# A block with two attentions: normed heads and squared activations kept in PSUM, V made tile by tile, two result banks

## The chip, the core and the metric

The kernel runs on one core of a Trainium2 chip. The metric is device time in microseconds (us) of one execution. TensorE (PE) multiplies and writes to PSUM, VectorE (DVE), ScalarE (ACT) and GpSimd (POOL) do the elementwise work, and SyncE (SP) starts the transfers. PSUM has 8 banks of 128 x 512 float32; GpSimd works in SBUF only.

## The reference

All values are float32, 512 tokens, width 1024. Cut to what matters here:

```python
# first block: layer 0 is a short convolution beside an attention, layer 1 a convolution module
def squared_relu_mlp(h, w1, w2):                 # once in each of the two layers, width 4096
    return jnp.square(jax.nn.relu(h @ w1)) @ w2

# second block: one layer, 16 meta tokens ahead of the 512
proj = _rmsnorm(h) @ w_in                        # q, k, v (8 heads of 64), forget gate, u (512)
q, k = _rmsnorm(q per head, q_norm_w), _rmsnorm(k per head, k_norm_w)
log_f = jax.nn.log_sigmoid(fg + b_fgate); cum_logf = jnp.cumsum(log_f)
s = q @ k.T * HEAD_DIM ** -0.5 + cum_logf[t] - cum_logf[s]     # causal
a_out = softmax(s) @ v                           # by query blocks of 128
pooled = trailing means of u over 2, 4, 8, 16 tokens, minus u   # one window per 128 columns
p_out = einsum(pooled, w_pool) * pool_scale
h = h + concat([a_out, p_out]) @ w_out
h = h + (silu(n2 @ w_gate) * (n2 @ w_up)) @ w_down              # width 2816
```

## The kernel before

**Layout.** Activations are held transposed: features on the 128 partitions, 512 tokens in the free dimension. A weight block is 8 tiles of 128 x 128. Each float32 operand is split into two parts of TensorE's rounded type (`wh`/`wl`, `XH`/`XL`, `HH`/`HL`, and so on): ScalarE or VectorE rounds (high part), and a subtraction gives the low part. A product is three matmuls (high x high, high x low, low x high; lines 1478 to 1480). A tile of 8 k-steps is 24 matmuls and fills one of the banks 0 to 3 in turn.

**Order.** It is written by hand, engine by engine, and held together by semaphores; each engine runs its own list in order. Weights pass through a ring of four slots: SP loads block n, ScalarE makes `wh` (`hi(n)`, which waits for the block n-3 counted by `blocks_done`), GpSimd makes `wl` (`lo_range`), PE multiplies. `bank_free` counts the tiles whose bank VectorE has read.

**The squared-ReLU MLP** (twice, each in two chunks of 16 tiles up and 8 down). For each up tile VectorE runs four instructions (lines 1207 to 1213): `tmp0 = PSUM * r2`; `tmp1 = max(tmp0, 0) * tmp0`; a cast `tmp1` to `HH`; `HL = tmp1 - HH`. The second half of the first down tile needs all 16 up tiles (`hid`).

**w_in_2** (the second block's input projection). Tiles 0 to 3 are q, 4 the forget gate, 5 to 8 u, 9 the first k tile; then the pool products (12 matmuls), then three k tiles, then V. A k or q tile is two heads. For head pair e: `head_in` scales the tile into `head_t`, ScalarE squares it, PE sums by head (`head_stat`, line 1779), ScalarE takes the root, VectorE inverts and spreads the factors (`hexp`), PE turns them into bank HB (`head_spread`, line 1788), and `head_norm` multiplies in place and writes both parts of both heads (`Q2H`, `Q2L`, `K2H`, `K2L`). `head_stat(e)` waits until pair e-1 is finished (`heads_done`). The hooks of `tile` put stats and spreads between the k-steps of a later tile. Tiles 4 to 9 and the k tiles also multiply the 16 meta tokens (48 short matmuls more). V runs k-step by k-step over four banks at once, and 20 matmuls without use (`keep_busy`) stand ahead of the attention.

**The second attention** runs in 32 units (head h, query block i) through a pipeline in which step s does scores(s), transposes unit s-3 (`turn`) and multiplies by V every other step (`values`). ScalarE: exponent of s, then copies of the transposed unit s-3, and for s = 9, 13, ... the copy `XH` of a finished head (line 755). VectorE: maximum, reciprocal, low parts, and `XL` of the head (line 937, followed by `yl_done`). GpSimd normalises. There is one result bank, so `values` of the next head waits for `yl_done`; the weights of the first four tiles of w_out_2 are made before it.

## Time and profile before

| | us |
|---|---|
| median of 3 runs (1941.9 to 1943.06) | 1942.8 |
| the profiled execution | 1945.64 |
| its span, first to last instruction | 1943.9 |
| PE busy (95% of the span) | 1848.9 |
| DVE, POOL, ACT busy | 1009.1, 921.5, 579.1 |

Matmuls are pipelined, and a row's duration includes the overlap: in a row of matmuls with 512 columns they start 0.23 us apart though each lasts 0.39. Stages of the span, in us: first attention about 180 to 246, MLP 0 about 300 to 490 in its first chunk, MLP 1 about 930 to 1110, w_in_2 about 1285 to 1453, the second attention 1457.9 to 1528.7, w_out_2 and the gated MLP from there.

### The profile page before, as it was taken

What the parts mean: (1) busy time and instruction counts of PE and PEld (TensorE: products, weight loads), DVE (VectorE), ACT (ScalarE), POOL (GpSimd) and SP (SyncE); (2) the same over time, 40 slices, a digit from 0 to 9 for tenths busy, and PEclk for the clock granted to TensorE, in tenths of its full rate; (3) what the DMA queues carried; (4) which work ended last, traced back from release to release, by engine and by line L of the source; (5) the groups of instructions that cost most, each with busy time, mean ns of one, the idle gap of its engine ahead of it and who ended that gap; (6) DMA issues with size and microseconds to landing.
All of it is one profiled execution on the core that took longest, in us unless ns stands there. A gap on an engine that the chain in (4) does not pass through costs nothing.

```text
span 1943.9 us, 23828 instructions
## 1 busy us (share of the span) xinstructions
PE 1848.9 (95%) x8563; PEld 1527.0 (79%) x8563; DVE 1009.1 (52%) x1330; ACT 579.1 (30%) x854; POOL 921.5 (47%) x482
## 2 busy tenths in 40 slices
PE   7897999999999999899999999999898999999999
PEld 5776977878888777677878888888778778888887
DVE  4886737820771479856770384257526335444300
ACT  4225714111111444344211111142126342222221
POOL 7345535434444469935534444452224354444442
PEclk9998999999999999999999999999889999999999
DMA  5152022323332213202322233321110023323332
GB/s 180 48 141 76 1 70 72 97 87 97 97 96 93 71 54 96 80 31 87 98 86 97 97 95 96 95 72 50 51 45 12 33 75 100 96 96 97 98 107 76
DMA packets 45782, 157.87 MB, mean 81 GB/s; under 512 B 5585, under 2 KB 5841, under 8 KB 45713
## 3 DMA queue, kind: packets, MB, share of 16 engines
q1 hardware_dynamic: 45712, 156.93, 25.6%
q8 instruction: 46, 0.75, 0.2%
q14 instruction: 24, 0.19, 0.0%
HBM read 152.58 MB, written 2.10 MB: 80 GB/s over the span
## 4 chain that ended last, share of the span: by engine, by line
PE 73%; DVE 17%; POOL 5%; issue 3%; ACT 1%; DMA 0%; DVEq 0%; SPq 0%; POOLq 0%; ACTq 0%
PE PS L1478 23%; PE PS L1479 22%; PE PS L1480 22%; DVE HL L937 2%; DVE tmp L945 2%; PE PS L1488 2%; POOL acc_p L519 2%; DVE HH L1211 2%; POOL wl L508 2%; DVE tmp L937 1%; DVE sqb L937 1%; PE PS L1649 1%; POOL acc_p L551 1%; PE PS L1508 1%; PE PS L1788 1%
## 5 line engine op out<-in xcount | busy, mean ns | idle before, releaser
L451 POOL TENSOR_TENSOR wl<-raw,wh 128x1024 fp32r<-128x1024 f32 x240 | 593.0, 2473 | 764.7 <-ACT wh L606 484.9
L1478 PE MATMUL PS<-XH,wh 128*128 128x512 f32 x1440 | 577.0, 401 | 32.0 <-DVE XL L945 16.2
L1479 PE MATMUL PS<-XL,wh 128*128 128x512 f32 x1440 | 566.7, 394 | 0.0
L1480 PE MATMUL PS<-XH,wl 128*128 128x512 f32 x1440 | 566.5, 393 | 0.0
L606 ACT ACTIVATE wh<-raw 128x1024 fp32r<-128x1024 f32 x152 | 161.1, 1061 | 668.1 <-PE PS L1480 668.1
L1478 PEld LDWEIGHTS PS<-XH,wh 128*128 128x128 f32 x1440 | 274.0, 190 | 100.8 <-issue 23.2
L1480 PEld LDWEIGHTS PS<-XH,wl 128*128 128x128 f32 x1440 | 273.9, 190 | 58.4
L1479 PEld LDWEIGHTS PS<-XL,wh 128*128 128x128 f32 x1440 | 274.3, 190 | 53.4
L1478 PE MATMUL PS<-HH,wh 128*128 128x512 f32 x688 | 269.6, 392 | 8.4 <-DVE HL L937 8.4
L1479 PE MATMUL PS<-HL,wh 128*128 128x512 f32 x688 | 269.1, 391 | 0.0
L1480 PE MATMUL PS<-HH,wl 128*128 128x512 f32 x688 | 268.8, 391 | 0.0
L937 DVE TENSOR_TENSOR tmp<-PS,r 128x512 f32<-128x512 f32 x126 | 86.8, 691 | 144.2 <-PE PS L1480 118.7
L1478 PEld LDWEIGHTS PS<-HH,wh 128*128 128x128 f32 x688 | 130.1, 189 | 36.5 <-POOL wl L451 9.2
L592 ACT ACTIVATE wh<-raw 128x1024 fp32r<-128x1024 f32 x94 | 98.5, 1055 | 195.9 <-PE PS L1480 179.9
L1480 PEld LDWEIGHTS PS<-HH,wl 128*128 128x128 f32 x688 | 130.1, 189 | 27.2
L1479 PEld LDWEIGHTS PS<-HL,wh 128*128 128x128 f32 x688 | 130.2, 189 | 26.8
L1211 DVE CAST HH<-tmp 128x512 f32 x64 | 110.2, 1721 | 9.6 <-DVE tmp L945 5.8
L1231 DVE COPY M<-PS 128x512 f32 x16 | 11.1, 692 | 158.4 <-PE PS L1480 158.4
L442 POOL TENSOR_TENSOR wl<-raw,wh 128x1024 fp32r<-128x1024 f32 x20 | 48.9, 2451 | 90.4 <-ACT wh L592 90.2
L916 ACT ACTIVATE wh<-raw 128x1024 fp32r<-128x1024 f32 x40 | 42.5, 1062 | 158.4 <-PE PS L1480 158.4
L472 POOL TENSOR_TENSOR prob<-prob,cols 128x512 f32<-128x512 f32 (+2 forms) x64 | 57.5, 900 | 66.6 <-DVE cols L1138 66.3
L937 DVE TENSOR_TENSOR X<-X,PS 128x512 f32<-128x512 f32 x16 | 11.0, 688 | 148.4 <-PE PS L1480 148.4
(277 smaller groups left out, 2326.8 us busy)
## 6 DMA issues: line engine op xcount, KB each, us to landing
raw<-weights SPq DMA_DIRECT2D x286, 512.0 KB, 3.5
X<-x_t SPq DMA_DIRECT2D x8, 256.0 KB, 6.8
out_t<-X SPq DMA_DIRECT2D x8, 256.0 KB, 4.6
KH<-rope_h SPq DMA_DIRECT2D x4, 128.0 KB, 4.5
KL<-rope_l SPq DMA_DIRECT2D x4, 128.0 KB, 5.4
QH<-XH SPq DMA_DIRECT2D x16, 32.0 KB, 2.0
QL<-XL SPq DMA_DIRECT2D x16, 32.0 KB, 2.0
pos_i<-positions SPq DMA_DIRECT2D x1, 256.0 KB, 8.2
```

The costliest lines, as they stand in the source:

```text
L442: pool.tensor_tensor(wl[:, n % RING], raw[:, n % RING], wh[:, n % RING].bitcast(F32), ALU.subtract).then_inc(w_lo, 1)
L451: pool.tensor_tensor(wl[:, j], raw[:, j], wh[:, j].bitcast(F32), ALU.subtract).then_inc(w_lo, 1)
L472: pool.tensor_tensor(p, p, cols[:, u % 4, 2:3].broadcast_to(p.shape), ALU.mult).then_inc(p_done, 1)
L508: pool.tensor_tensor(wl[:, i % RING], raw[:, i % RING], wh[:, i % RING].bitcast(F32), ALU.subtract).then_inc(w_lo, 1)
L592: sc.activation(wh[:, j], raw[:, j], ACT.Copy).then_inc(w_hi, 1)
L606: sc.activation(wh[:, j], raw[:, j], ACT.Copy).then_inc(w_hi, 1)
L916: sc.activation(wh[:, slot], raw[:, slot], ACT.Copy).then_inc(w_hi, 1)
L937: return v.tensor_tensor(out, a, b, op)
L1211: v.tensor_copy(HH[:, g * 4 + j], tmp[:, 1]).then_inc(dve, 1)
L1478: pe.matmul(out, wa, xa, start=start, stop=False)
L1479: pe.matmul(out, wa, xb, start=False, stop=False)
L1480: return pe.matmul(out, wb, xa, start=False, stop=stop)
```

## The change

1. **MLPs.** ScalarE keeps the square of `r2` (only for entries x1 and x3). VectorE: `tmp0 = PSUM * r2`; `x = max(PSUM, 0) * tmp0`, written to PSUM (banks 6 and 7 in turn), which frees the tile's bank; ScalarE copies `x` to `HH`; VectorE: `HL = x - HH`. ScalarE's loop holds the weight's `hi` and the `HH` copy in turn.
2. **Heads.** `head_norm` is split in three: `head_factor`, `head_norm` (one multiplication that leaves the normed pair in bank HB, `head_n`) and `head_low`. ScalarE writes the high parts (`head_round`), VectorE only the low parts. `head_stat(e)` waits for `head_n`, `head_spread(e)` for `heads_done` of pair e-1. VectorE's list interleaves these with the forget gate and the pool tiles; the low parts of the pooled tiles go to GpSimd.
3. **w_in_2 order.** The second k tile moves ahead of the pool products; hooks move.
4. **V** is made one tile after the other, the meta product after the second; `v_done` releases each. The 20 matmuls and the wait for all four V tiles ahead of the attention are gone.
5. **Attention.** Results alternate between banks 6 and 7; the small transposed part moves to the bank of the main part, or to bank 5.
6. **w_out_2.** Its first four `hi` and `lo` are put into the attention, at steps 13, 17, 21 and 25 of ScalarE and ahead of GpSimd's units 12, 16, 20 and 24.

```diff
+W_OUT_2_STEPS = (13, 17, 21, 25)
+        def squared(j):
+            return PS[:, (HB, META_BANK)[j % 2]]
-                    PS[0:META, (5, 7)[u % 2], 0:P])
+            small = PS[0:META, 5, 0:P] if i == 3 else PS[0:META, (4, 1)[u % 2], S - (i % 2 + 1) * P:S - i % 2 * P]
-            return 6 + h % 2 if layer == 0 else 6
+            return 6 + h % 2
# gpsimd, normalise(layer)
+                    if layer == 1 and u + 1 in W_OUT_2_STEPS:
+                        n = BLOCK0["w_out_2"] + W_OUT_2_STEPS.index(u + 1)
+                        lo_range(n, n + 1)
# gpsimd, w_in_2
-            lo_range(BLOCK0["w_in_2"] + 4, BLOCK0["w_in_2b"] + 7)
+            for t in range(4):
+                lo_range(BLOCK0["w_in_2"] + (9 + t if t else 4), BLOCK0["w_in_2"] + 10 + t)
+                pool.wait_ge(pool_hi, t + 1)
+                pool.tensor_tensor(pool_l[:, t], pooled[:, t], pool_h[:, t].bitcast(F32), ALU.subtract)
...
# scalar
+                form = ACT.Square if entry in ("x1", "x3") else ACT.Copy
+                    if layer == 1 and s in W_OUT_2_STEPS:
+                        hi(BLOCK0["w_out_2"] + W_OUT_2_STEPS.index(s))
+                    if c == 0:
+                        for j in range(4):
+                            sc.wait_ge(bank_free, T0 + j + 1)
+                            sc.activation(HH[:, j], squared(j), ACT.Copy).then_inc(hid_hi, 1)
+                    with sc.Fori(1 if c == 0 else 0, CHUNK // 4, 1) as g:
...
+                            sc.activation(wh[:, slot], raw[:, slot], ACT.Copy).then_inc(w_hi, 1)
+                            sc.wait_ge(bank_free, g * 4 + (T0 + j + 1))
+                            sc.activation(HH[:, g * 4 + j], squared(j), ACT.Copy).then_inc(hid_hi, 1)
+            def head_round(e):
+                sc.wait_ge(head_n, e + 1)
+                for odd in range(2):
+                    sc.activation(H[:, tokens], PS[:, HB], ACT.Copy, scale=own).then_inc(head_hi, 1)
# vector, mlp
-                            tt(tmp[:, 0], PS[:, (T0 + j) % 4], r2[:], ALU.mult).then_inc(bank_free, 1)
-                            stt(tmp[:, 1], tmp[:, 0], 0.0, tmp[:, 0], ALU.max, ALU.mult).then_inc(dve, 1)
-                            v.tensor_copy(HH[:, g * 4 + j], tmp[:, 1]).then_inc(dve, 1)
-                            tt(HL[:, g * 4 + j], tmp[:, 1], f(HH[:, g * 4 + j]), ALU.subtract).then_inc(hid, 1)
+                            tt(tmp[:, 0], z, r2[:], ALU.mult).then_inc(dve, 1)
+                            stt(x, z, 0.0, tmp[:, 0], ALU.max, ALU.mult).then_inc(bank_free, 1)
+                            v.wait_ge(hid_hi, g * 4 + (h0 + j + 1))
+                            tt(HL[:, g * 4 + j], x, f(HH[:, g * 4 + j]), ALU.subtract).then_inc(hid, 1)
# tensor
-                    ring = 2 if layer == 0 else 1
+                    ring = 2
-                    pe.wait_ge(heads_done, e)
+                    pe.wait_ge(head_n, e)
+                if e:                                  # head_spread
+                    pe.wait_ge(heads_done, e)
-                     6: {2: head(2)[0], 6: head(2)[1]}, 7: {4: head(3)[0], 7: head(3)[1]}}
+                     6: {2: head(2)[0], 7: head(2)[1]}, 7: {4: head(3)[0]}, 8: {2: head(3)[1]},
+                     10: {3: head(4)[0], 6: head(4)[1]}}
-            keep_busy(W_START[1], PS[:, HB])
...
```

In the MLP, VectorE's list per up tile. Before:

```order
L937 TENSOR_TENSOR tmp<-PS,r 128x512
L1208 REGISTER_ALU
L945 SCALAR_TENSOR_TENSOR tmp<-tmp 128x512
L1210 ISA
L1211 ISA
L1211 COPY HH<-tmp 128x512
L1212 REGISTER_ALU
L937 REGISTER_ALU
L937 TENSOR_TENSOR HL<-tmp,HH 128x512
```

After:

```order
L999 TENSOR_TENSOR tmp<-PS,r 128x512
L1269 REGISTER_ALU
L1007 SCALAR_TENSOR_TENSOR PS<-PS,tmp 128x512
L1271 REGISTER_ALU
L999 ISA
L999 TENSOR_TENSOR HL<-PS,HH 128x512
```

The copy to `HH` has left this list, and the last two instructions now work on PSUM. In w_in_2, ScalarE's list from the second square of head pair 1 on (`hcol<-PS` is the root, `logf` the forget gate). Before:

```order
L830 ACTIVATE head_q<-head_t 128x512
L837 ACTIVATE hcol<-PS 128x8
L592 ACTIVATE wh<-raw 128x1024
L830 ACTIVATE head_q<-head_t 128x512
L837 ACTIVATE hcol<-PS 128x8
L592 ACTIVATE wh<-raw 128x1024
L857 ACT_TABLE_LOAD
L857 ACTIVATE logf<-logf 8x528
L860 ACT_TABLE_LOAD
L860 ACTIVATE logf<-logf 8x528
```

After:

```order
L868 ACTIVATE head_q<-head_t 128x512
L892 ACTIVATE Q2H<-PS,headones 128x512 x2
L612 ACTIVATE wh<-raw 128x1024
L900 ACT_TABLE_LOAD
L900 ACTIVATE logf<-logf 8x528
L903 ACT_TABLE_LOAD
L903 ACTIVATE logf<-logf 8x528
L875 ACT_TABLE_LOAD
L875 ACTIVATE hcol<-PS 128x8
L868 ACTIVATE head_q<-head_t 128x512
```

The root of head pair 1 stood ahead of the forget gate and now stands behind it, with three table loads in between. In the second attention, ScalarE's list at step 17 (a unit's exponent, the copies of an earlier unit, the finished head). Before:

```order
L743 ACTIVATE P2H<-PS 128x2x128
L729 ACTIVATE prob_102,cols<-PS,cols 128x272
L742 ACTIVATE PMH<-PS 16x128
L743 ACTIVATE P2H<-PS 128x3x128
L755 ACTIVATE XH<-PS 64x512
L729 ACTIVATE prob_102,cols<-PS,cols 128x400
```

After:

```order
L750 ACTIVATE prob_102,cols<-PS,cols 128x272
L763 ACTIVATE PMH<-PS 16x128
L764 ACTIVATE P2H<-PS 128x3x128
L612 ACTIVATE wh<-raw 128x1024
L778 ACTIVATE XH<-PS 64x512
L750 ACTIVATE prob_102,cols<-PS,cols 128x400
```

A weight block's `hi` stands between the copies and the head's copy, at four of the eight heads.

## Rows read from the trace of the kernel before

**Rows 1.** The page: busy time, share of the span and instructions of each engine.
```profile
PE 1848.9 (95%) x8563; PEld 1527.0 (79%) x8563; DVE 1009.1 (52%) x1330; ACT 579.1 (30%) x854; POOL 921.5 (47%) x482
```

**Rows 2.** PE's waits over the whole span: total us, times, longest.
```profile
PE PS L1478 <- DVE HL L937: 8.4, 2, 4.2
...
PE PS L1488 <- DVE XL L937: 5.0, 7, 1.4
```

**Rows 3.** Timeline of DVE and ACT, MLP 0: start, duration, instruction, idle before.
```profile
306.37 0.76 DVE L945 SCALAR_TENSOR_TENSOR PS<-M,vec,PS 128x512 f32<-128x512 f32 x1
...
323.43 0.69 DVE L937 TENSOR_TENSOR tmp<-PS,r 128x512 f32<-128x512 f32 x1 [4.22 <-ACT r L623]
...
325.01 2.39 DVE L1211 CAST HH<-tmp 128x512 f32 x1 [0.15 <-DVE tmp L945]
327.52 2.68 DVE L937 TENSOR_TENSOR HL<-tmp,HH 128x512 f32 x1
...
336.77 0.43 DVE L1211 CAST HH<-tmp 128x512 f32 x1
...
306.30 0.59 ACT L641 ACTIVATE X<-PS 128x512 f32<-128x512 f32 x1
```

**Rows 4.** Windows: start:end, length, busy us of PE, PEld, DVE, ACT, POOL, granted clock, DMA.
```profile
1303.90:1457.90 154.00, 139.81 (x721) 117.22 (x720) 77.24 (x120) 31.51 (x48) 38.36 (x20) 0.90 0.16 53
...
1340.00:1348.00 8.00, 5.95 (x30) 5.37 (x29) 5.61 (x9) 1.06 (x1) 0.97 (x2) 0.79 0.00 0
...
400.00:404.00 4.00, 3.11 (x7) 2.48 (x8) 0.74 (x1) 0.00 (x0) 0.19 (x1) 0.59 0.39 131
1010.30:1016.00 5.70, 5.67 (x15) 4.52 (x16) 0.00 (x0) 0.00 (x0) 0.00 (x0) 0.58 0.29 92
1457.90:1528.70 70.80, 60.20 (x472) 56.60 (x473) 45.83 (x140) 41.33 (x141) 25.62 (x33) 1.00 0.03 9
```

**Rows 5.** Timeline of PE in w_in_2, rows with idle time, and the 20 matmuls.
```profile
1314.17 1.02 PE L1779 MATMUL PS<-headones,head_q 128*128 128x2 f32 x8 [0.80 <-DVE Q2L L945]
...
1342.73 2.06 PE L1788 MATMUL PS<-ident,hexp 128*128 128x128 f32 x8 [2.05 <-DVE hexp L1343]
...
1452.79 4.69 PE L1488 MATMUL PS<-ident_r 128*128 128x512 f32 x20
1457.88 0.30 PE L1478 MATMUL PS<-K2H,Q2H 128*128 128x144 f32 x1 [0.40 <-DVE VML L937]
```

**Rows 6.** Timeline of ACT at the forget gate.
```profile
1325.31 1.06 ACT L592 ACTIVATE wh<-raw 128x1024 fp32r<-128x1024 f32 x1
1326.38 1.28 ACT L857 ACT_TABLE_LOAD   x1
1327.67 0.65 ACT L857 ACTIVATE logf<-logf 8x528 f32<-8x528 f32 x1
...
1330.81 1.28 ACT L837 ACT_TABLE_LOAD   x1
1336.61 0.18 ACT L837 ACTIVATE hcol<-PS 128x8 f32<-128x8 f32 x1 [4.52 <-PE PS L1779]
```

**Rows 7.** Timeline of DVE and POOL at the prefix sums.
```profile
1338.83 2.42 DVE L1382 CAST decay<-logf 8x528 fp32r<-8x528 f32 x1
...
1337.82 3.14 POOL L451 TENSOR_TENSOR wl<-raw,wh 128x1024 fp32r<-128x1024 f32 x1 [8.96 <-ACT wh L592]
```

**Rows 8.** Timeline of ACT, DVE and PE, one head of the second attention.
```profile
1499.36 0.59 ACT L755 ACTIVATE XH<-PS 64x512 fp32r<-64x512 f32 x1
...
1499.98 0.69 DVE L937 TENSOR_TENSOR XL<-PS,XH 64x512 fp32r<-64x512 f32 x1 [0.56 <-ACT XH L755]
...
1502.25 0.67 DVE L937 TENSOR_TENSOR P2L<-PS,P2H 128x512 fp32r<-128x512 f32 x1
...
1502.98 0.28 PE L1652 MATMUL PS<-ident,prob 128*16 128x128 f32 x1 [0.26 <-DVE P2L L937]
```

**Rows 9.** Timeline of POOL at the start of the second attention.
```profile
1456.88 2.37 POOL L442 TENSOR_TENSOR wl<-raw,wh 128x1024 fp32r<-128x1024 f32 x1 [7.12 <-ACT wh L592]
```

More of the change, by code:

```diff
@@ L81 @@
     _PHASES += [(f"mlp1_up{_c}", CHUNK, CHUNK), (f"mlp1_down{_c}", 8 * CHUNK // SLOTS, 8)]
-_PHASES += [("w_in_2", 10, 10), ("pool", 1, 4), ("w_in_2b", 7, 7), ("w_out_2", 8, 8), ("ffn_up", 2 * HT2, 2 * HT2), ("ffn_down", 24, 8)]
+_PHASES += [("w_in_2", 11, 11), ("pool", 1, 4), ("w_in_2b", 6, 6), ("w_out_2", 8, 8), ("ffn_up", 2 * HT2, 2 * HT2), ("ffn_down", 24, 8)]
 BLOCK0, TILE0 = {}, {}
@@ L443, in lo @@
                                        ALU.subtract).then_inc(w_lo, 1)
-                while a % RING:
+                while a < b and a % RING:
                     lo(a)
@@ L1399, in pool_tile, with pool_out @@
                     pooled_done, i + 1)
-            def pool_lo_part(i):
-                v.wait_ge(pool_hi, i + 1)
-                tt(pool_l[:, i], pooled[:, i], f(pool_h[:, i]), ALU.subtract).then_inc(pool_lo, 1)
+            def pool_out():
+                for i in range(4):
+                    T = TILE0["pool"] + i
+                    v.wait_ge(blocks_done, BLOCK0["pool"] + 1)
+                    sig(ts(p_out(i), PS[:, T % 4], col("pool_scale", i), ALU.mult), bank_free, T + 1)
             for e in range(4):
                 head_in(e, "w_in_2", e)
+            head_factor(0)
             head_norm(0)
+            log_forget()
+            head_low(0)
+            head_factor(1)
             head_norm(1)
-            log_forget()
+            pool_tile(0)
+            head_low(1)
+            prefix_sums()
+            head_factor(2)
             head_norm(2)
-            pool_tile(0)
-            prefix_sums()
+            pool_tile(1)
+            head_low(2)
+            head_factor(3)
+            pool_tile(2)
             head_norm(3)
-            for i in range(1, 4):
-                pool_tile(i)
-                pool_lo_part(i - 1)
-            pool_lo_part(3)
+            head_low(3)
+            pool_tile(3)
             head_in(4, "w_in_2", 9)
-            for i in range(4):
-                T = TILE0["pool"] + i
-                v.wait_ge(blocks_done, BLOCK0["pool"] + 1)
-                sig(ts(p_out(i), PS[:, T % 4], col("pool_scale", i), ALU.mult), bank_free, T + 1)
+            head_factor(4)
             head_norm(4)
-            for e in range(5, 8):
-                head_in(e, "w_in_2b", e - 5)
-                head_norm(e)
+            head_in(5, "w_in_2", 10)
+            head_low(4)
+            pool_out()
+            head_factor(5)
+            head_norm(5)
+            head_in(6, "w_in_2b", 0)
+            head_low(5)
+            head_factor(6)
+            head_norm(6)
+            head_in(7, "w_in_2b", 1)
+            head_low(6)
+            head_factor(7)
+            head_norm(7)
+            head_low(7)
             v.wait_ge(decay_q, 16 * HEADS)
@@ L1429, in _, with v_low @@
                 v.wait_ge(loaded, 16 * 2)
-            for t in range(4):
-                T = TILE0["w_in_2b"] + 3 + t
+            def v_low(t):
+                T = TILE0["w_in_2b"] + 2 + t
                 lo_n[0] += 1
@@ L1940, in _pack_weights @@
     put(n0 + 9, 0, t[0])
+    put(n0 + 10, 0, t[1])
     n0 = BLOCK0["w_in_2b"]
-    for i in range(1, 4):
-        put(n0 + i - 1, 0, t[i])
+    for i in range(2, 4):
+        put(n0 + i - 2, 0, t[i])
     t = _tiles(v, KT, 4)
     for k_tile in range(KT):
-        put(n0 + 3 + k_tile // 2, 4 * (k_tile % 2), t[:, k_tile])
+        put(n0 + 2 + k_tile // 2, 4 * (k_tile % 2), t[:, k_tile])
     put(BLOCK0["pool"], 0, w_pool_2[0])
```

187 lines of the change are left out of this document (118 added, 69 removed).

## The prediction, made before the changed kernel ran

> **What bounds the kernel now.** I read the page first: PE is busy for 1848.9 of 1943.9 us [rows 1], so a faster VectorE or ScalarE is worth nothing by itself, and the change can only give back three things: time in which PE waits, matmuls that do no work, and time in which PE runs at half its clock. Then the list of PE's waits [rows 2], and for each of them the place in PE's timeline, because each stage has a limit of its own. Last the windows, for the granted clock behind each wait [rows 4].
>
> Three stages are touched. In the MLPs PE waits for `HL` twice, 4.2 us each, once per MLP, at the second half of the first down tile. In w_in_2, from the first head stat at 1303.9 to the attention at 1457.9, PE waits nine times; [rows 5] holds the first, the fourth longest and the last of them (0.80, 2.05, 0.40), and the nine come to 14.2 us. In the second attention PE waits for `XL` seven times, 5.0 us in all.
>
> **MLPs.** VectorE starts the first tile at 323.43, when four tiles are already made, and then takes 0.69 + 0.69 us plus a cast and a subtraction. Those two work in SBUF alone. The cast takes 0.43 us where GpSimd is idle and 2.39 where it makes a weight's low part, and the subtraction is stretched to 2.68 likewise [rows 3]. About 4.8 us a tile against PE's 5.5 (24 matmuls, 0.23 apart) never makes up the lag, and that is the 4.2 us. After the change every VectorE instruction has one operand in PSUM: 0.69, then 0.76 (the same form, `PS<-M,vec,PS`), then 0.69, with ScalarE's copy from PSUM (0.59) between [rows 3]. With hand-offs of about 0.1 that is some 3.1 to 3.2 us a tile. VectorE gains 2.3 us a tile on PE, has caught up by about tile 7, and PE doesn't wait at the down tile. That returns 2 x 4.2 = 8.4 us. Behind each wait the clock stands at half: 0.59 granted over 400 to 404 with 3.11 us busy, which is 1.6 us lost, and 0.58 over 5.7 us behind the other, 2.4 us lost [rows 4]. PE doesn't stop there any more, so I count those 4.0 too. A bank is now freed by the second VectorE instruction, 0.76 us later: the fifth up tile may wait some 0.35 us for it, while a wait of 1.0 one tile later, for a bank that the slow VectorE held, goes. Over two MLPs that is +1.3. Together 13.7 us; between 9 (the waits alone) and 15. ScalarE's extra copies (64 x 0.59) lie in its idle time: its `hi` for the fourth tile ahead stands before the copy, so a weight is late only if VectorE is more than two tiles late.
>
> The Trainium skill ("VectorE: DVE Perf Modes", Rules for kernel authors) says of elementwise work on a matmul's output to accept the slower rate from PSUM, or to copy to SBUF first where many operations follow, and this change does the opposite. By that rule alone the old cast of 0.43 is the better one, and the MLP term would be near nought. The rows put 2.39 beside it in the same loop, and they decide for me.
>
> **w_in_2.** I make a ledger of the 154.0 us from 1303.9 to 1457.9: 14.2 waits, 4.7 for the 20 matmuls [rows 5], and 15.4 of clock (mean 0.90 granted [rows 4]). 119.7 us are work, which the change leaves alone: nine tiles, twelve pool products, 120 matmuls for V, eight stats and spreads.
>
> What is new in it: `head_stat(e)` needs only the normed pair in PSUM, and `head_in` of the next pair comes before the low parts. For a k pair the chain behind a tile's end is 0.9 (`head_in`) + 0.65 (square) to the stat, whose slot is 2.1 us behind that end; then root, low parts of the pair before (2 x 0.76 and four short ones, 2.3 us) and the factors (1.1) end about 5 us behind the tile, and the spread's slot is at 6.4. So the k pairs run without a wait, which takes away two waits of 3 us each and the half clock behind them, most of the 15.4. V tile by tile needs no four free banks at once (2.7 us), and the evacuation of three V tiles lies beside later ones, so the attention starts when the last V tile ends.
>
> Three stalls remain or come. (1) The root of pair 1 is now behind the forget gate. VectorE has the gate's argument ready about 2.2 us behind tile 4, at 1314.0; ScalarE then does exp, a table load, ln, a table load and the root: 0.65 + 1.28 + 0.65 + 1.28 + 0.18 and hand-offs. The first load is not on this chain: a load is done before its instruction's wait, as the one at 1330.81 for a root at 1336.61 shows [rows 6]. Root at 1319.1, factors 0.65, spread possible at 1319.8; its slot is at 1318.1. Stall 1.7. (2) The factors of pair 2 stand behind pool tile 0, low parts of pair 1 and the prefix sums. From the end of tile 5 at 1323.5: 2.5 for the pool tile and about 2 more because GpSimd makes a weight then, 1.5 low parts, then 5.1 for the prefix sums if the cast takes 0.43 where it took 2.42 under GpSimd's work [rows 7]: 1334.2 with the factors. The slot is at 1331.1. Stall 3.1, and the clock falls behind it as it did behind the 2.05 us (0.79 over 8 us, 1.7 lost [rows 4]). (3) The first tile behind the pool products still waits for the banks of `p_out`, 1.3. Sum 7.8. All other slots have over 1 us to spare, except the last V weights, which come at the moment they are needed.
>
> 119.7 + 7.8 = 127.5 against 154.0: 26.5 us less. Bounds: 33 if the two new stalls are not there and small waits go too; 15 if the clock falls behind each new stall for as long as it did over 1384 to 1424.
>
> The skill ("ScalarE: Activation LUTs", What ACT_TABLE_LOAD costs) adds a drain of about 1.38 us to each 1.28 us load, so 2.66 a switch. By that the first stall would be some 3 to 4 us longer. Here exp starts 0.01 us behind its load, and the load 0.01 behind the weight ahead of it [rows 6]: no drain is to be seen.
>
> **The second attention.** The `XL` waits look like 5.0 us to be had, and I don't count them. One head takes 8.1 us, and the chain that closes it is ScalarE's `XH` at 1499.36, VectorE's `XL` at 1499.98 (it waited for that), the low parts of two units behind it, the last 2.92 us later, and PE's transpose that waits for those at 1502.98 [rows 8]. VectorE works without a break there. `XL` stays in VectorE's list with one bank or two, so PE only swaps its wait for `XL` for a longer one at the transpose. Only at the end, where nothing is queued behind, about 1.2 us come back.
>
> On that chain, between ScalarE's copies and `XH`, now stands a weight's high part, 1.06 us [rows 6], at four heads: +4.3. GpSimd's low part, 2.37 us [rows 9], ahead of units 12, 16, 20 and 24 delays their normalisation until just when the chain, already later, asks for it; at worst another 1.3 each. The start: the last V tile's high part (0.6) and then the table load (1.28 [rows 6]) are now behind the last V matmul, where the 20 matmuls covered them: +1.0. Sum +4.3 +1.0 -1.2 = 4.1 us more. Bounds: 3 us less (if the seven waits mostly go and the copies fit in ScalarE's gaps) to 10 more.
>
> **Elsewhere** nothing moves: blocks, transfers and the gated MLP are as before, and the first four weights of w_out_2 are ready in time either way.
>
> **Sum.** 13.7 + 26.5 - 4.1 = 36.1 us. The profiled execution took 1945.64 us, 1.74 outside its span; less 36.1 it is 1909.5. It lay 2.8 above the median of 1942.8, so the prediction for the median is 1906.7, say 1907.
>
> **Rivals.**
> A. The attention gives the 5 us instead of taking 4, and the prefix sums don't stall PE: the XL waits are PE's only waits of size there, and ScalarE has gaps of 1 to 2 us in each head. Against it stands the closed chain. 13.7 + 31.5 + 3 gives 1895. Chance 20%.
> B. w_in_2 gets back only about half: VectorE's list is now nearly full between 1311 and 1365, many of its instructions read SBUF twice and are stretched by GpSimd, which has four subtractions more, and every stall over 2 us costs the clock as well. 13.7 + 15 - 7 gives 1921. Chance 22%.
> C. Slower: in the MLP ScalarE's `hi` now stands behind a copy that waits for VectorE, so weights, VectorE and PE form a ring. It decides when a tile's VectorE chain exceeds PE's 5.5 us; it needs 0.35 us above that in each of 64 tiles to eat the other 22 us. If the PSUM forms were stretched by GpSimd as the SBUF ones are (2.0 each for two of them), the chain is 7.2 us, 64 x 1.7 = 109 us, less 22: near 2030. The rows with a PSUM operand all read 0.69 to 0.76, which is against it. Chance 3%.
> D. The change does less than it says: removed waits come back one step later for small reasons, and the time is within a few us of before. For it speaks only that the attention already works so. 1939. Chance 3%.
>
> **The numbers.** Forecast 1907 with 52%, A 20%, B 22%, C 3%, D 3%. The forecast's own range is 1901 to 1914; with most of A and B, 1894 to 1922. A difference of 0.2% (3.9 us) is about what a measurement of this kernel tells from none. Faster 0.95, same 0.015, slower 0.035.
>
> **What will show it.** MLPs: no PE wait for `HL`, VectorE's three instructions at 0.7 to 0.8 whatever GpSimd does, granted clock 1.00 behind 400 and 1010. w_in_2: waits of PE for `hexp` at two spreads of q pairs, about 1.7 and 3.1 us, none for `head_q`; about 127 us from the first stat to the first scores. Attention: PE's waits for `XL` gone and those for `P2L` grown, about 75 us in place of 70.8, with the longer heads at the four steps that hold a weight. Wrong if VectorE's PSUM forms take over 1 us, if the k pairs still wait, or if the attention gets shorter.

## The result

| | median us | runs |
|---|---|---|
| before | 1942.35 (1940.52 to 1943.06) | 4 |
| after | 1924.42 (1922.97 to 1926.59) | 4 |

The ratio is 0.991, 95% interval 0.9893 to 0.9927: faster by about 18 us, where 1907 had been predicted, with 1901 to 1914 as the forecast's own range and 1894 to 1922 with most of the rivals. The direction was right; half of the gain didn't come, and the time lies outside both ranges. The profiled execution of the changed kernel took 1925.12 us, its span 1923.1, so 20.8 less than the span of before. By stages of the span:

| | before | after | measured | predicted |
|---|---|---|---|---|
| the stretches that hold MLP 0 and MLP 1 | 461.2, 465.5 | 454.7, 458.0 | -14.0 | -13.7 |
| w_in_2, first head stat to first scores | 154.0 | 131.2 | -22.8 | -26.5 |
| second attention | 70.8 | 86.3 | +15.5 | +4.1 |
| start, and all behind the attention | | | +0.5 | 0 |
| sum | | | -20.8 | -36.1 |

The page's first line, against [rows 1]. VectorE gave up 158 us and ScalarE took 47.

```profile
PE 1839.2 (96%) x8543; PEld 1522.5 (79%) x8543; DVE 850.6 (44%) x1262; ACT 626.0 (33%) x934; POOL 917.2 (48%) x486
```

PE's waits over the span (total, times, longest), against [rows 2]: the two rows of [rows 2] are gone from the list (of the waits for an `XL` only those of other stages are left), and its second row now is that for GpSimd's `prob`.

```profile
PE PS L1749 <- POOL prob L487: 8.4, 4, 2.8
...
PE PS L1887 <- DVE hexp L1402: 4.8, 2, 3.2
...
PE PS L1749 <- DVE P2L L999: 2.7, 3, 1.3
```

**MLP.** The timeline of VectorE and ScalarE in MLP 0, the place of [rows 3]. VectorE's three instructions take 0.69, 0.70 and 0.69 us; the middle one lies between 0.698 and 0.700 us in all 64 tiles, beside GpSimd's work or not. In the kernel before, the cast took 1.72 us on average over MLP 0 and the subtraction 1.01.

```profile
322.55 0.69 DVE L999 TENSOR_TENSOR tmp<-PS,r 128x512 f32<-128x512 f32 x1 [4.22 <-ACT r L644]
323.28 0.70 DVE L1007 SCALAR_TENSOR_TENSOR PS<-PS,tmp 128x512 f32<-128x512 f32 x1
325.56 0.69 DVE L999 TENSOR_TENSOR HL<-PS,HH 128x512 f32 x1 [1.59 <-ACT HH L798]
...
324.83 0.58 ACT L798 ACTIVATE HH<-PS 128x512 fp32r<-128x512 f32 x1
```

**w_in_2.** PE's three waits over 0.3 us, against the nine that [rows 5] samples:

```profile
1304.99 2.08 PE L1887 MATMUL PS<-ident,hexp 128*128 128x128 f32 x8 [1.63 <-DVE hexp L1402]
1321.28 1.45 PE L1887 MATMUL PS<-ident,hexp 128*128 128x128 f32 x8 [3.19 <-DVE hexp L1402]
1368.56 0.47 PE L1571 MATMUL PS<-XH,wh 128*128 128x512 f32 x1 [1.66 <-DVE tmp L1003]
```

**Second attention.** ScalarE, GpSimd and PE at the first head that holds a weight block:

```profile
1447.90 1.04 ACT L612 ACTIVATE wh<-raw 128x1024 fp32r<-128x1024 f32 x1
1448.97 0.59 ACT L778 ACTIVATE XH<-PS 64x512 fp32r<-64x512 f32 x1
...
1449.02 2.36 POOL L454 TENSOR_TENSOR wl<-raw,wh 128x1024 fp32r<-128x1024 f32 x1 [6.11 <-ACT wh L612]
1451.34 2.28 POOL L487 TENSOR_TENSOR prob<-prob,cols 128x144 f32<-128x144 f32 x3
...
1452.36 0.37 PE L1749 MATMUL PS<-ident,prob 128*16 128x128 f32 x1 [2.80 <-POOL prob L487]
```

GpSimd stands 6.11 us in front of its subtraction, because ScalarE makes `wh` only at step 13. Units 12 to 14 wait behind that subtraction; when it ends they are normalised in one go (x3), and PE has stood still for 2.80 us. The same happens at 1464.15, 1475.07 and 1485.69 with 1.84, 1.86 and 1.86 us.

The windows (start:end, length, busy us of PE, PEld, DVE, ACT, POOL, granted clock, DMA), against [rows 4]:

```profile
400.00:404.00 4.00, 4.00 (x20) 3.30 (x19) 0.69 (x1) 1.06 (x1) 2.33 (x1) 1.00 0.32 122
...
1289.00:1420.10 131.10, 124.62 (x700) 105.32 (x700) 69.48 (x115) 35.76 (x58) 34.63 (x20) 0.96 0.15 50
...
1420.10:1506.40 86.30, 70.08 (x473) 67.18 (x472) 46.86 (x141) 46.73 (x146) 33.65 (x36) 0.84 0.08 25
...
1452.00:1460.00 8.00, 7.64 (x43) 7.68 (x43) 3.58 (x13) 2.85 (x12) 2.69 (x4) 0.59 0.22 68
```

Behind the MLP's old wait the clock is whole again, 1.00 for 0.59. The attention had 1.00 over its whole length before and has 0.84 now; in the 8 us behind the wait of 2.80 it is 0.59, that is mostly 1.2 GHz and not 2.4.

### The profile page after: what moved, and what is told of

Read it like the earlier page. It is cut to its first block, busy times and chain, and to the rows that moved or that the text cites. A ratio compares the mean times of both kernels' runs of the same rounds, so it can differ in the third digit from the quotient of the medians.

```text
span 1923.1 us, 23732 instructions
## 1 busy us (share of the span) xinstructions
PE 1839.2 (96%) x8543; PEld 1522.5 (79%) x8543; DVE 850.6 (44%) x1262; ACT 626.0 (33%) x934; POOL 917.2 (48%) x486
## 4 chain that ended last, share of the span: by engine, by line
PE 82%; DVE 7%; POOL 6%; issue 3%; ACT 2%; DMA 0%; SPq 0%; POOLq 0%; DVEq 0%; ACTq 0%
PE PS L1571 26%; PE PS L1573 25%; PE PS L1572 25%; PE PS L1581 2%; POOL acc_p L534 2%; POOL wl L523 2%; DVE sqb L999 1%; PE PS L1746 1%; POOL acc_p L566 1%; DVE PS L1007 1%; PE PS L1601 1%; DVE ssq L999 1%; PE PS L1613 1%; PE PS L1887 1%; POOL wl L454 0%
## 5 line engine op out<-in xcount | busy, mean ns | idle before, releaser
L463 POOL TENSOR_TENSOR wl<-raw,wh 128x1024 fp32r<-128x1024 f32 x232 | 564.5, 2435 | 699.2 <-ACT wh L626 309.2
L454 POOL TENSOR_TENSOR wl<-raw,wh 128x1024 fp32r<-128x1024 f32 x28 | 68.6, 2456 | 129.5 <-ACT wh L612 129.4
L1290 DVE COPY M<-PS 128x512 f32 x16 | 11.1, 691 | 158.6 <-PE PS L1573 158.6
L496 POOL TENSOR_TENSOR ssq<-ssq,sqb 128x512 f32<-128x512 f32 x42 | 58.0, 1381 | 47.6 <-ACT sqb L672 45.8
```

Of the source, the lines that this page charges most:

```text
L454: pool.tensor_tensor(wl[:, n % RING], raw[:, n % RING], wh[:, n % RING].bitcast(F32), ALU.subtract).then_inc(w_lo, 1)
L463: pool.tensor_tensor(wl[:, j], raw[:, j], wh[:, j].bitcast(F32), ALU.subtract).then_inc(w_lo, 1)
L496: pool.tensor_tensor(ssq[:], ssq[:], sqb[:, k % 2], ALU.add).then_inc(ssq_adds, 1)
```

## The experiments

The question was the attention: 11 us more than predicted. Three explanations stood: GpSimd's order, ScalarE's copy in the head's chain, the second bank. Each kernel below is a change to the changed kernel unless it says otherwise. Its median is given beside a median of before taken together with it, with the ratio's interval. All stage lengths are from one profiled execution each. "hi" is ScalarE's copy `wh`, "lo" GpSimd's subtraction `wl`.

### Lo behind the normalisation

```diff
-                    if layer == 1 and u + 1 in W_OUT_2_STEPS:
-                        n = BLOCK0["w_out_2"] + W_OUT_2_STEPS.index(u + 1)
+                    if layer == 1 and u in W_OUT_2_STEPS:
+                        n = BLOCK0["w_out_2"] + W_OUT_2_STEPS.index(u)
```

> One change against the changed kernel: in the second attention GpSimd's subtraction for the low part of w_out_2 is recorded behind the normalisation of units 12, 16, 20 and 24, not ahead of it; ScalarE's copies for the high part stay where they are. Theory 1 (GpSimd's order: a normalisation that is ready stands behind a subtraction that waits for ScalarE's copy, and the clock falls behind each such wait): TensorE's four waits for GpSimd (8.4 us in the kernel after) shrink to about 1 each or less, since the next unit's normalisation is the one that now stands behind the subtraction and has a whole head's slack, the granted clock of the stage rises from 0.84 to over 0.92, and the attention takes 74 to 78 us in place of 86.3; the time falls by 8 to 12 us to 1912 to 1916. Rival 1 (what costs is ScalarE's copy of about 1.06 on the head's closed chain, four times): the order on GpSimd changes nothing in the sum, under 2 us. Rival 2 (the second result bank costs the stage its time): nothing either.

1923.08 against 1943.21 (0.9865 to 0.9911). The waits for GpSimd are gone, but those for `P2L` rose from 2.7 to 10.8 us (12 times), and the attention takes 81.5 us. ScalarE, VectorE and PE at the same head, and the window of the stage:

```profile
1454.58 1.04 ACT L612 ACTIVATE wh<-raw 128x1024 fp32r<-128x1024 f32 x1
1455.65 0.59 ACT L778 ACTIVATE XH<-PS 64x512 fp32r<-64x512 f32 x1
...
1456.27 0.69 DVE L999 TENSOR_TENSOR XL<-PS,XH 64x512 fp32r<-64x512 f32 x1 [2.02 <-ACT XH L778]
...
1457.80 0.28 PE L1749 MATMUL PS<-ident,prob 128*16 128x128 f32 x1 [1.56 <-DVE P2L L999]
...
1426.80:1508.30 81.50, 65.92 (x474) 62.97 (x472) 46.34 (x141) 46.95 (x146) 33.80 (x36) 0.90 0.08 27
```

That is the chain of the prediction with hi in it: hi, `XH`, `XL`, low parts, transpose. So GpSimd's order is not the cause. With lo moved, the wait changes its name: this head now waits 1.56 us for `P2L` and another 1.55 at 1460.13, where it waited 2.80 for GpSimd. Over the stage PE's waits for GpSimd and `P2L` at the transposes are 10.8 us against 11.1 (8.4 + 2.7). The 4.8 us by which the stage is shorter than 86.3 are no gain of the new order: the granted clock is 0.90 here and 0.84 there, and two kernels further down with the unchanged attention took 82.0 and 83.0 us at 0.90.

### Hi one step earlier as well

```diff
-                    if layer == 1 and s in W_OUT_2_STEPS:
-                        hi(BLOCK0["w_out_2"] + W_OUT_2_STEPS.index(s))
+                    if layer == 1 and s + 1 in W_OUT_2_STEPS:
+                        hi(BLOCK0["w_out_2"] + W_OUT_2_STEPS.index(s + 1))
```

(with the edit above. The texts written before the runs call it "one head earlier"; it is one step of the unit pipeline, a quarter of a head, from s = 13 to s = 12 and so on, which puts hi ahead of the step that closes the head)

> As the run before (the low part behind the normalisation), and ScalarE's copy for the high part one head earlier, so that GpSimd never waits for it. Theory 1: the subtraction then begins as soon as GpSimd comes to it, so the next unit's normalisation is not late either; all waits for GpSimd are gone, the attention takes 71 to 75 us and the time is 1909 to 1913, 0 to 3 us under the run before. Rival 1: ScalarE's copy is still on the chain, four times 1.06 and the clock with it; the attention stays above 82 us. If Theory 1 holds with the chain of the prediction as well, what is left above the 70.8 us of the kernel before is about 4 us.

1918.84 against 1943.21 (0.9834 to 0.9891); the attention takes 74.6 us at 0.95, and PE's waits for `P2L` at the transposes are 7.0 us, 3.8 less than in the run before, close to four copies of 1.04. The stage length is that of Theory 1, the time is not: w_in_2, with the same code as after, took 137.1 us here and not 131.2 (see below).

### Hi earlier, lo left ahead

> One change against the changed kernel, the fourth corner of the two moves: ScalarE's copy for the high part one head earlier, GpSimd's subtraction still ahead of the normalisation of units 12, 16, 20 and 24. Measured so far, attention and granted clock: late copy, subtraction ahead 86.3 at 0.84 (82.0 at 0.90 in a second run of the same stage); late copy, subtraction behind 81.5 at 0.90; early copy, subtraction behind 74.6 at 0.95 and 72.5 at 0.98. Theory (what costs is the copy in the head's chain and GpSimd's wait for it; the subtraction itself finds room as soon as its input is there): 72 to 76 us, no wait for GpSimd over 0.5, time 1912 to 1919. Rival (the subtraction's own 2.37 us ahead of a normalisation costs): one wait for GpSimd at each of four heads, 1 us or more each, and 78 us or more.

1910.49 against 1944.87 (0.9803 to 0.9878), a little under the time expected; attention 73.6 us at 0.95, no wait for GpSimd. ScalarE and GpSimd:

```profile
1442.16 1.04 ACT L612 ACTIVATE wh<-raw 128x1024 fp32r<-128x1024 f32 x1
...
1443.28 2.39 POOL L454 TENSOR_TENSOR wl<-raw,wh 128x1024 fp32r<-128x1024 f32 x1 [1.13 <-ACT wh L612]
1445.61 1.04 POOL L487 TENSOR_TENSOR prob<-prob,cols 128x144 f32<-128x144 f32 x2
```

Lo now begins at 1443.28, and unit 12 is normalised before PE asks for it. The four corners (us, granted clock):

| | lo ahead | lo behind |
|---|---|---|
| hi at the head's copy | 86.3 (0.84), 82.0 (0.90), 83.0 (0.90) | 81.5 (0.90) |
| hi one step earlier | 73.6 (0.95) | 74.6 (0.95), 72.5 (0.98) |

Of the kernels in the table, those with 82.0, 83.0 and 72.5 also have the stalls of w_in_2 filled or removed (below). The place of hi decides, by one step of the pipeline. The place of lo is worth nothing once hi is early, and at the same clock of 0.90 it is worth 0.5 to 1.5 us where hi is late.

### The waits of the attention filled with matmuls

```diff
+                    if layer == 1 and u + 1 in W_OUT_2_STEPS:
+                        keep_busy(8, PS[:, (4, 1)[u % 2]])
                     pe.wait_ge(p_done, U0 + u + 1)
```

> One change against the changed kernel: ahead of TensorE's wait for the weights of units 12, 16, 20 and 24 in the second attention stand eight matmuls whose results nobody reads (about 1.7 us in all at full clock), so that the engine works where it would wait; the order on GpSimd is left as it is. It tells how much of the loss is the wait and how much the clock behind it. Theory 1a (most of the loss is the clock: the waits for GpSimd add up to 8.4 us, half of which are hidden in the slack of the chain, and the granted clock of 0.84 costs 13.8): the clock goes to over 0.93, the waits that are left are under 0.5 each, and the time falls by 4 to 8 us though not one wait of the chain is removed. Theory 1b (the loss is the wait alone, the clock's fall is hidden in other engines' time): the clock rises and the time stays within 2 us.

1928.01 against 1943.21 (0.9888 to 0.9943). The clock rose to 0.96, but the stage took 83.0 us. The fillers begin only behind the wait for `P2L` and take 2.1 us where the wait left to fill was shorter, which would push the loop back each time. That decided neither way, and it was run again with five, on the kernel without the stalls of w_in_2 (further down), whose attention is the changed one:

> The kernel with the two stalls of w_in_2 removed (the second attention as in the changed kernel, so it is entered without a stall before it), and 5 matmuls without use ahead of TensorE's wait for the weights of units 12, 16, 20 and 24. In the earlier run with 8 of them the fillers took 2.12 us each where, behind the wait for P2L, only some 1.1 to 1.2 us of waiting for GpSimd were left, so they pushed the head loop back; the stage took 83.0 us at a granted clock of 0.96. Without fillers it took 82.0 at 0.90. Five take about 1.1 each. Theory (the clock is part of the loss and the wait the other): the clock stays at 0.95 or more, the waits for GpSimd are under 0.4 each, and the stage takes 77 to 80 us; time 1910 to 1913. Rival (the clock's fall costs nothing here, since the head loop is closed by the other engines): 81 to 83 us at the higher clock, time 1915 or more.

1909.23 against 1945.29 (0.9793 to 0.9848), with the four runs at 1904.25 and 1906.09 (granted clock 0.992 over the whole span) and at 1912.37 and 1912.77 (0.987). The profile is of the run of 1906.09. The filler and the window of the attention, with five fillers, then the window of the kernel that differs only in having none:

```profile
1440.55 1.43 PE L1581 MATMUL PS<-ident_r 128*128 128x512 f32 x5 [1.57 <-DVE P2L L999]
...
1410.90:1489.70 78.80, 65.98 (x493) 61.32 (x492) 47.10 (x141) 46.63 (x146) 33.73 (x36) 0.98 0.09 28
...
1412.90:1494.90 82.00, 65.72 (x474) 62.86 (x472) 46.83 (x141) 46.81 (x146) 33.65 (x36) 0.90 0.08 27
```

78.8 us at 0.98: with the order of the change still in place, fillers where PE waited for GpSimd, and the clock kept. Without fillers it took 82.0 at 0.90, and the changed kernel 86.3 at 0.84. With hi early it is 72.5 at 0.98. So the 15.5 us fall into three: 72.5 - 70.8 = 1.7 for the rest of the change, 78.8 - 72.5 = 6.3 for the waits, and 86.3 - 78.8 = 7.5 for the clock behind them, in the execution profiled (3.2 and 4.2 in two others of the same attention code). The fillers may still push the loop, so 6.3 can be too much and 7.5 too little.

The windows give the split another way. PE runs the same 472 to 474 matmuls in each kernel without fillers. It was busy for 60.2 us in the kernel before and not busy for 10.6; in the changed kernel 70.1 and 16.2. The same matmuls took 9.9 us longer at the lower clock, and only 5.6 us were added in which PE stood. Where hi is late PE stands for 15.6 to 16.9 us, whatever the place of lo; where it is early, for 11.0 to 12.6. By either count the clock is the largest part in the changed kernel's profile; in the two of the same attention at 0.90 it is about as large as the waits (busy 5.5 and 5.9 us more than before, not busy 5.7 and 6.3 more).

### One result bank again

```diff
-            return 6 + h % 2
+            return 6 + h % 2 if layer == 0 else 6
-                    ring = 2
+                    ring = 2 if layer == 0 else 1
```

(with hi earlier and lo behind)

> The run with hi one head earlier and lo behind the normalisation, and with one result bank in the second attention as in the kernel before (bank 6 for every head, TensorE waits for yl_done of the head just finished). It tests the prediction's claim that the waits for XL (5.0 us before) are not on the chain that closes the head loop (XH, XL, low parts, transposes). Theory (claim right): XL waits come back with 4 to 6 us and the waits for P2L shrink by as much; the attention takes 73 to 77 us against 74.6 at a granted clock of 0.95, the time is within 2 us of the run with two banks. Rival (the second bank is worth its waits): the attention takes 4 to 6 us more at the same clock.

1911.66 against 1942.02 (0.9821 to 0.9861). Waits of PE in the attention, and its window:

```profile
PE PS L1581 <- DVE XL L999: 5.0, 7, 1.4
...
PE PS L1749 <- DVE P2L L999: 2.7, 5, 0.9
...
1420.90:1494.50 73.60, 62.58 (x473) 59.09 (x471) 46.42 (x141) 46.86 (x146) 33.60 (x36) 0.95 0.09 29
```

With two banks the waits are 6.7 to 7.0 for `P2L` at the transposes and 1.6 behind the last one, none for `XL`, and the stage takes 72.5 to 74.6. The prediction's claim holds: the 5.0 us of waits that [rows 2] shows are not to be had by a second bank.

### The splits behind the attention

```diff
# gpsimd
-                    if layer == 1 and u + 1 in W_OUT_2_STEPS:
-                        n = BLOCK0["w_out_2"] + W_OUT_2_STEPS.index(u + 1)
-                        lo_range(n, n + 1)
...
-            lo_range(BLOCK0["w_out_2"] + 4, BLOCK0["ffn_up"] + 4)
+            lo_range(BLOCK0["w_out_2"], BLOCK0["ffn_up"] + 4)
# scalar
-                    if layer == 1 and s in W_OUT_2_STEPS:
-                        hi(BLOCK0["w_out_2"] + W_OUT_2_STEPS.index(s))
...
-            hi_range(n0 + 22, BLOCK0["ffn_up"] + 4)
+            hi_range(n0 + 18, BLOCK0["ffn_up"] + 4)
```

> The changed kernel with the first four splits of w_out_2 taken out of the attention altogether: ScalarE makes them after its last head copy and GpSimd after its last normalisation; the rest of the attention (two banks, the moved small part, V by tiles) is as changed. Theory (all that the attention lost is due to the splits standing in it): it takes 67 to 71 us, at or below the 70.8 of before, with no wait for GpSimd; TensorE then waits 2 to 4 us for the first block of w_out_2 (1.06 and 2.37 one behind the other, partly beside the last head), and the clock falls there; the time is 1909 to 1914. Rival (the second bank or the small part costs the stage): the attention stays above 75.

1916.59 against 1942.02 (0.9844 to 0.9881), over the time expected. Counted with the 1.46 us of issue that end it in every other kernel, the attention took 74.9 us at 0.95. PE then stood for 4.39 us before w_out_2 in place of that 1.46, waiting for the first `wl`. The 67 to 71 us were wrong: without any split in it the stage is as long as with well placed ones, so these cost nothing. What is above 70.8 is in part the clock (PE busy 62.4 us for 60.2) and the start (1.2); the rest was not taken apart.

### The two stalls of w_in_2 removed

```diff
# scalar
+            head_root(1)
             sc.wait_ge(fz, 1)
...
-            head_root(1)
             head_square(2)
# vector
+            head_factor(2)
             prefix_sums()
-            head_factor(2)
```

> One change against the changed kernel, in the two stalls of w_in_2: ScalarE's square root for the second pair of heads stands ahead of its work on the forget gate, and VectorE's factors for the third pair ahead of its prefix sums. Theory (the two waits of TensorE for the spread, 1.63 and 3.19 us, are queue order on ScalarE and VectorE, and the granted clock of 0.79 and 0.72 behind them comes from them): both waits fall under 0.5 us, the stage from the first head's statistics to the first scores goes from 131.15 to 123 to 125 us, and the time falls by 6 to 8 us. Rival (the forget gate's or the prefix sums' own results are asked for at once, so the wait moves to them): a new wait of 1.5 to 3 us stands within 15 us behind the old ones, and the time falls by under 3.

1915.33 against 1943.21 (0.9842 to 0.9875). Both stalls are gone, nothing takes their place, and the stage is 10 us shorter, more than expected:

```profile
1291.70:1412.90 121.20, 119.54 (x700) 101.22 (x700) 67.20 (x115) 35.76 (x58) 35.01 (x20) 1.00 0.17 54
```

### The same two stalls filled

```diff
             def head_spread(e):
+                if e in (1, 2):
+                    pe.wait_ge(bank_free, T0 + 4 + e)
+                    keep_busy(7 * e, PS[:, meta_bank(T0 + 3 + e)])
```

> One change against the changed kernel: 7 matmuls without use ahead of TensorE's wait for the spread of pair 1 and 14 ahead of that of pair 2 in w_in_2 (about 0.22 us each: 1.5 and 3.1 us, as long as the waits), nothing reordered. It separates a wait from what the clock does behind it. With the waits as they are the stage took 131.1 us at 0.96 (130.3, 130.9 in two others) or 137.0 at 0.89 (in three runs), with the waits removed 121.2 at 1.00. Theory (a wait of 1.63 is enough to bring the clock down, and that is most of the loss): the clock is 1.00 throughout, the fillers take the waits' place, and the stage takes 125 to 127 us; the time is 1917 to 1920 and does not scatter as before. Rival (the clock falls for another reason than the waits, or the lost time is the waits' own): the clock stays at 0.96 or less, or the stage stays above 129.

1918.38 against 1944.87 (0.9846 to 0.9879), as expected, and the four runs lie within 1.0 us (1918.17 to 1919.17), where the runs of the changed kernel spread over 3.6. The window:

```profile
1289.80:1416.20 126.40, 124.74 (x721) 105.01 (x721) 69.20 (x115) 35.76 (x58) 34.77 (x20) 1.00 0.16 52
```

126.4 - 121.2 = 5.2 us is the price of the waits (1.63 + 3.19 = 4.8 in PE's list), and 131.1 - 126.4 = 4.7 that of the clock behind them.

### The MLP part alone, on the kernel before

The edit is the diff's `squared`, `keep_r2`, and the loops of `mlp` on ScalarE and VectorE, nothing else.

> The kernel before with the MLP part of the change alone (squared activations in PSUM, ScalarE copies to HH, the square of r2 kept); all else as before. Theory: this part is worth what the traces show, 14.0 us in the two MLP stages and nothing behind them, so the time is 1927 to 1930. Rival (part of its gain in the whole change comes from, or is lost to, what the other parts do to the clock or to the weights' ring): under 11 or over 17.

1928.87 against 1942.02 (0.9908 to 0.9942), 13.2 us by the medians: the part is worth what it was counted for, and its attention takes 70.8 us at 1.00 as before.

### Both repairs

> The changed kernel with both repairs: hi of w_out_2 one head earlier and lo behind the normalisation in the attention, and in w_in_2 the root of pair 1 ahead of the forget gate and the factors of pair 2 ahead of the prefix sums. Theory (the two losses are independent): w_in_2 takes 121 to 122 us (121.2 with its repair alone), the attention 72 to 75 (74.6 with its repair alone at a granted clock of 0.95), and the time is 1905 to 1910, under both of the repairs alone (1915.3 and 1918.8) and at what was predicted for the change itself. Rival (what the one gains the clock takes back in the other): above 1912.

1902.49 against 1942.02 (0.9782 to 0.9815), below the range expected, and 22 us below the changed kernel's 1924.42. w_in_2 and the attention:

```profile
1289.70:1411.00 121.30, 119.64 (x701) 101.26 (x701) 67.20 (x115) 35.78 (x58) 35.02 (x20) 1.00 0.17 54
1410.90:1483.40 72.50, 60.28 (x474) 57.65 (x472) 46.55 (x141) 46.95 (x146) 33.58 (x36) 0.98 0.09 30
```

### The start of the attention

Two edits on top of it: an exponent of one column ahead of V's first copy, for the table load; then VectorE's low part of the last V tile behind the maxima of units 0 and 1.

> The kernel with both repairs, and an exponent of one column whose result nobody reads ahead of ScalarE's first copy of V, so that the table load for the exponent (1.28 us, with 1.07 behind it before the first softmax row's result) stands beside V and not between V and the attention. Theory: TensorE's wait for the first prob (1.69 us in every run so far, against 0.48 in the kernel before) falls to about 0.5, the attention from 72.5 to 70.5 to 71.5 us, and the time is 1900 to 1902 against 1902.5. Rival (the copies of V, not the table, are what comes last): the wait stays above 1.3 and the time is the same.

1903.95 against 1944.87 (0.977 to 0.9802): the rival. The load was early and nothing was gained: PE's wait for the first `prob` was 1.60 us for 1.69, and the attention took 74.1 us at 0.94. ScalarE and VectorE:

```profile
1394.77 1.28 ACT L945 ACT_TABLE_LOAD   x1
...
1413.51 0.38 ACT L750 ACTIVATE prob<-PS,cols 128x144 f32<-128x144 f32 x1 [1.23 <-DVE cols L1196]
...
1412.38 0.75 DVE L1008 SCALAR_TENSOR_TENSOR V2L<-PS,rcol,V2H 128x512 fp32r<-128x512 f32 x1 [4.69 <-ACT V2H L710]
1413.17 0.66 DVE L1196 TENSOR_REDUCE cols<-PS 128x1 f32<-128x144 f32 x2
```

The maximum stands behind `V2L`, and `V2L` behind ScalarE's `V2H`.

> The kernel with both repairs and the early table load, and VectorE's low part of the last V tile recorded behind the maxima of units 0 and 1 of the attention and not ahead of them. In the run before, the wait for the first prob stayed at 1.60 us: the table was there, and ScalarE waited 1.23 for the maximum, which stood on VectorE behind that low part (it waits for ScalarE's copy of the V tile and takes 0.75 itself). Theory (VectorE's order sets the start of the attention): the first maximum comes 1.0 to 1.3 us earlier, TensorE's wait for prob falls to 0.3 to 0.6, the attention takes 70.8 to 72 us at a granted clock of 0.98 or more, and the time is 1900 to 1902, 1 to 3 under the 1902.5 and 1904 of the two kernels before it. Rival (the copy of V on ScalarE stands in the same place and is what comes last): a wait of 1.0 or more stays and the time is the same.

1902.57 against 1943.16 (0.9781 to 0.9808, five runs). PE's wait is 0.49:

```profile
1414.04 0.45 PE L1573 MATMUL PS<-K2H,Q2H 128*128 128x400 f32 x1 [0.49 <-ACT prob L750]
```

The wait fell as expected, the time didn't: the attention took 73.4 us at 0.95, the clock having fallen to 0.79 over 1432 to 1448, behind waits of 1.29 for `P2L` that all these kernels have. The three kernels (0.9799, 0.9786, 0.9794) can't be told apart. Any of them is the version that beats both: about 40 us under before and 22 under the change.

## Why the prediction was wrong, step by step

**MLPs: right.** 14.0 for 13.7. No wait for `HL`; the middle instruction takes 0.70 for 0.76; the clock is 1.00 behind 400. Alone it gave 13.2 by the medians. The prediction said that the change does the opposite of the Trainium skill's rule ("VectorE: DVE Perf Modes", Rules for kernel authors). That is too strong: the rule gives two ways, to accept the rate of PSUM or to copy to SBUF first where many operations follow, and the change takes the first. The second is in effect what the kernel before did from its second instruction on, and here it was the slower one: its forms were stretched, and with an operand in PSUM nothing was.

**w_in_2: mechanism right, one size off.** Of the ledger's three stalls, 1.7, 3.1 and 1.3, the trace has 1.63, 3.19 and 1.66. The k pairs wait for nothing. Off was the clock: I had counted 1.7 us behind the second stall alone and none behind the first, by the row of 0.79 behind 2.05 us. It cost 4.7, and in the profiles of three sister kernels about 10. In the changed kernel the first stall of 1.63 us brought the clock down as well.

The 1.7 of the first stall is right in part by luck. The prediction holds that the first table load is not on its chain, and then has 1.1 us more between 1314.0 and 1319.1 than its terms add up to (4.0), called hand-offs. ScalarE and VectorE in the changed kernel:

```profile
1298.79 1.28 ACT L900 ACT_TABLE_LOAD   x1
1300.09 0.64 ACT L900 ACTIVATE logf<-logf 8x528 f32<-8x528 f32 x1
...
1298.52 0.70 DVE L1007 SCALAR_TENSOR_TENSOR logf<-logf 8x528 f32<-8x528 f32 x1
```

The argument is ready at 1299.22 and the load ends at 1300.07, so 0.85 us of it are on the chain, and true hand-offs are next to nothing. The loads themselves went as read: each is followed by its instruction 0.01 us later, and the drain that the Trainium skill ("ScalarE: Activation LUTs", What ACT_TABLE_LOAD costs) adds is not there, or the stall of 1.63 would have been over 4.

**Second attention: the failed step.** It is the term of the attention, "Sum +4.3 +1.0 -1.2 = 4.1 us more": it measured +15.5. The path was right, ScalarE's copy in the chain that closes a head. The sum left out, without a reason, what the clock would cost behind the longer waits, and that was its largest part.

1. The clock was counted at nothing. In the MLPs and in w_in_2 I had counted half clock behind waits of 2.05 us and more; here I lengthened the waits at four heads and left the clock at the 1.00 of before. It was 0.84, and cost 7.5 us by the run with fillers, 9.9 by PE's busy time for the same matmuls.
2. The waits were nearly right. PE stood for 5.6 us more than before where 4.1 had been summed. Of these, hi late against hi early makes 3.8 to 4.4 in PE's list of waits, against the 4.3 of the four copies (4 x 1.04 measured). By the run with fillers the waits are 6.3.
3. "GpSimd's low part ... at worst another 1.3 each", counted at nothing, held as a price though not as a picture. GpSimd's subtraction did stand between hi and the normalisation, and PE's list shows 8.4 us for GpSimd. But with lo moved away the same waits stood under the name `P2L`, and at the same clock the stage was 0.5 to 1.5 us shorter, not 8.
4. The 1.2 us at the end didn't come: the last wait for `XL` (1.44) became one for `P2L` (1.61). The start cost 1.2, PE's wait for the first `prob` growing from 0.48 to 1.69, for 1.0; but its cause was VectorE's order and not the table load alone.

What held is the reason not to count the `XL` waits. Where hi is off the chain and the clock is kept, the stage takes 72.5, where the prediction without the copy's 4.3 would have had 70.6.

**Rivals.** B had nearly the right size (1921) for the wrong place: it put 11.5 us of the loss into w_in_2, which lost 3.7 of 26.5, and 2.9 into the attention, which lost 11.4. Its remark that stalls cost the clock as well is what the forecast lacked. A is refuted by the result and by the run with one bank, C by the 0.70 us, D by the result.

## What to carry to other kernels

An operation of two engines (one rounds, the other subtracts) put into a closed loop cost here what its first half added to the chain that closes the loop, and nothing one step earlier; place that half by the loop's slack, not by where there is a gap for it. Whoever adds waits like those of this case (1.3 to 3.2 us) to TensorE in a stage that ran at full clock should add a clock term as well, here as large as the waits themselves or larger. When a wait is named after one engine, move that and see whether another name takes over: here it was GpSimd, then `P2L`, and ScalarE's copy was the cause of both.

## What the runs showed of the hardware

How long TensorE stays at 1.2 GHz behind the same wait differs from profile to profile. w_in_2 with the same instructions took 131.1, 130.3, 130.9 and 130.2 us in four kernels and 137.0, 137.1 and 137.0 in three. Windows behind the wait of 1.63 us, in the kernel with lo behind:

```profile
1304.00:1312.00 8.00, 6.37 (x26) 5.69 (x25) 1.39 (x3) 2.83 (x5) 0.00 (x0) 0.57 0.13 50
1312.00:1320.00 8.00, 8.00 (x26) 6.84 (x26) 6.88 (x7) 2.27 (x4) 3.94 (x2) 0.50 0.22 67
1320.00:1328.00 8.00, 8.00 (x30) 7.13 (x30) 3.79 (x7) 0.00 (x0) 0.00 (x0) 0.50 0.01 2
1328.00:1336.00 8.00, 8.00 (x27) 6.80 (x26) 4.96 (x5) 2.32 (x3) 2.67 (x1) 0.51 0.00 0
...
1289.80:1426.80 137.00, 133.71 (x701) 113.17 (x700) 70.06 (x115) 35.64 (x58) 34.66 (x20) 0.89 0.15 48
```

PE is busy without a break over 1312 to 1336 and yet gets half its clock, for some 30 us in all; the next stall, 3.19 us in the changed kernel, disappears in the slow stretch. In the changed kernel the clock was 0.79 over 1304 to 1312 and back at 1.00 over 1312 to 1320. In two kernels, the one with one bank and the one with hi earlier and lo left ahead, it did not fall behind the same first wait. The window of the second of them, whose wait of 1.64 us ends at 1305.15:

```profile
1304.00:1312.00 8.00, 6.85 (x44) 6.19 (x45) 4.31 (x7) 3.86 (x8) 1.83 (x1) 1.00 0.06 25
```

And the same wait of 1.69 us at the attention's start was followed by 0.79 over 8 us in one kernel (1416 to 1424, the stalls of w_in_2 removed) and by 1.00 in another (1432 to 1440, hi and lo apart).

The three long profiles come from one chip, and three of the four short ones from two others, so a share of the chip is not ruled out. But executions of one kernel on one chip differ too: 1910.6 to 1922.0 us at granted clocks of 0.987 to 0.978 with hi and lo apart, on the chip of the long profiles, and 1909.3 to 1923.1 us, again 0.987 to 0.978, with hi earlier and lo left ahead, on another.

The Trainium skill ("TensorE: Matmul & The Clock Gate", Part 1) calls the slow start of a kernel "run-variable"; these profiles say nothing of the start, but show the like for a fall in the middle. So two single profiles can differ by 6 us in a stage whose code is the same. The four kernels in which both stalls of w_in_2 are removed and the attention has no fillers spread over 1.6 to 4.7 us, the one with filled stalls over 1.0, the one with fillers in the attention over 8.5, and the changed kernel and its variants that keep the stalls over 3.6 to 13.8. The price of a wait should therefore be given as a range, from the wait alone to the wait and half a clock over tens of microseconds.
